# Softmax denominators of an attention stage: adding two steps in float32 before one ones-matmul, with four probability buffers instead of two

## The reference, cut to what matters

```python
def latent_attention(q, k_lat, v_lat, k_ctx, v_ctx):
    scale = 1.0 / math.sqrt(HEAD_DIM)
    k_all = jnp.concatenate([k_ctx, k_lat], axis=1)   # (B, CTX+S, K, d)
    v_all = jnp.concatenate([v_ctx, v_lat], axis=1)
    ...
        s = jnp.einsum('bkgqd,bskd->bkgqs', q_blk, k_all).astype(jnp.float32) * scale
        p = jax.nn.softmax(s, axis=-1).astype(v_all.dtype)
        return jnp.einsum('bkgqs,bskd->bkgqd', p, v_all)
...
        attn = jax.nn.silu(ga) * latent_attention(q, k, v, kc, vc)   # (B, S, ATTN_WIDTH)
        conv = conv_branch(b, cg, hh, gc, conv_w[layer])              # (B, S, CONV_WIDTH)
        y = jnp.concatenate([attn, conv], axis=-1) @ w_out[layer]
        x = x + gate[:, None, :] * y
    return rms_norm(x, final_norm_g)
```

## Time and profile before

| | us |
|---|---|
| runs shown, median | 1207.76 (1199.58 to 1208.54) |
| fastest run shown | 1199.58 |
| span of the profiled execution (slowest core, 7) | 1199.1 |
| spans of its eight cores | 1184.6 to 1199.1 |
| attention stage on core 7, first to last exponential | 722 to 1062 |
| busy in the span: PE, DVE, ACT, POOL | 959.8, 429.3, 505.6, 173.2 |

### The profile page before, as it was taken

The page is one execution under the profiler, slowest core; times in us unless marked ns, Lnnn a source line. Parts: engine busy times, 40 slices in busy tenths (PEclk is TensorE's granted clock), DMA queues, the critical chain, the costliest instruction groups (busy, mean ns, idle before and its releaser), DMA issues.

```text
span 1199.1 us, 16921 instructions; the slowest of 8 cores (1184.6 to 1199.1 us)
## 1 busy us (share of the span) xinstructions
PE 959.8 (80%) x5604; PEld 456.6 (38%) x5604; DVE 429.3 (36%) x782; ACT 505.6 (42%) x902; POOL 173.2 (14%) x180
## 2 busy tenths in 40 slices
PE   0011249796898999999999998798989989889995
PEld 0011125443454444444444443343434334334442
DVE  0000134734756840222222223344444444424554
ACT  0000156435545421000000009699999899942111
POOL 1011002343325520011111110100000000000000
PEclk9999969898899999999999999899999999999998
DMA  9999995595549528888888408810000000021442
GB/s 155 158 157 158 151 165 126 84 226 89 88 72 131 81 36 106 105 106 106 106 106 106 71 1 133 130 20 1 1 1 1 1 1 1 1 106 71 156 174 93
DMA packets 101029, 107.30 MB, mean 89 GB/s; under 512 B 4176, under 2 KB 94672, under 8 KB 98768
## 3 DMA queue, kind: packets, MB, share of 16 engines
q0 software_dynamic: 80640, 73.44, 45.0%
q1 hardware_dynamic: 20304, 32.78, 8.8%
HBM read 171.26 MB, written 8.39 MB: 150 GB/s over the span
## 4 chain that ended last, share of the span: by engine, by line
PE 61%; DMA 25%; DVE 5%; ACT 4%; issue 3%; POOL 1%; DVEq 0%; POOLq 0%; ACTq 0%; SPq 0%
PE PS L818 14%; PE PS L976 9%; DMA R<-w_mod 9%; PE PS L937 8%; PE PS L891 8%; DMA big<-xT 6%; PE PS L915 5%; PE PS L789 5%; DMA wg<-w_mod 4%; DMA R<-w_out 4%; PE PS L707 3%; PE PS L473 3%; DMA R<-w_in 2%; PE PS L465 2%; PE PS L602 1%
## 5 line engine op out<-in xcount | busy, mean ns | idle before, releaser
L927 ACT ACTIVATE work<-PS,smx 128x1024 bf16<-128x1024 f32 x272 | 291.2, 1113 | 21.7 <-DVE work L942 11.7
L818 PE MATMUL PS<-R 128*128 128x512 bf16 x1024 | 228.6, 378 | 0.0
L942 DVE TENSOR_TENSOR work<-work 128x512 bf16<-128x512 bf16 x272 | 127.9, 472 | 170.2 <-ACT work L927 109.3
L937 PE MATMUL PS<-work,V 128*128 128x512 bf16 x544 | 164.3, 384 | 8.8 <-DVE work L902 4.4
L891 PE MATMUL PS<-big,KT 128*128 128x512 bf16 x544 | 163.9, 383 | 0.2 <-ACT work L838 0.2
L818 PEld LDWEIGHTS PS<-R 128*128 128x128 bf16 x1024 | 97.9, 97 | 117.8
L915 PE MATMUL PS<-work,ones_bf 128*128 128x512 bf16 x272 | 104.2, 383 | 30.2 <-DVE work L942 30.1
L976 PE MATMUL PS<-R,big 128*128 128x512 bf16 x512 | 112.5, 383 | 3.9 <-POOL big L907 3.9
L351 PE MATMUL PS<-s_bf,R 128*128 128x2 bf16 x512 | 14.8, 165 | 112.5 <-DMA R<-w_mod 112.5
L473 PE MATMUL PS<-R,big 128*128 128x512 bf16 x384 | 90.6, 391 | 0.0
L833 DVE TENSOR_TENSOR work<-PS,work 128x512 f32<-128x512 f32 x16 | 11.1, 692 | 202.9 <-PE PS L818 177.8
(11 more groups left out here) (118 smaller groups left out, 987.0 us busy)
## 6 DMA issues: line engine op xcount, KB each, us to landing
R<-w_mod POOLq DMA_DIRECT2D x8, 2048.0 KB, 24.1
R<-w_conv POOLq DMA_DIRECT2D x8, 2048.0 KB, 23.2
big<-xT POOLq DMA_DIRECT2D x6, 2048.0 KB, 24.1
big<-xT SPq DMA_DIRECT2D x2, 4096.0 KB, 24.8
wg<-w_mod POOLq DMA_DIRECT2D x8, 1024.0 KB, 25.0
R<-w_out POOLq DMA_DIRECT2D x4, 2048.0 KB, 15.3
big<-xown SPq DMA_DIRECT2D x8, 1024.0 KB, 4.9
out<-big SPq DMA_DIRECT2D x8, 1024.0 KB, 4.2
```

Of the source, the lines that this page charges most:

```text
L818: P.op("tensor", lambda e, wb4=wb4, kc=kc, g=g, tt=tt, b=b: e.matmul(bank(b), wb4[:, kc, g, :], hT_own[:, kc, tt * 512:(tt + 1) * 512], st ...
L927: P.op("scalar", lambda e, sp=sp, pp=pp: e.activation(out=PT[pp], in_=PS[sp][:], func=AF.Exp, scale=sm_scale, bias=smx[:, 2:3]), reads=[ps ...
L937: P.op("tensor", lambda e, ob=ob, chunk=chunk, g=g, pp=pp, cl=cl: e.matmul(bank(ob), V[:, chunk, g * 128:(g + 1) * 128], PT[pp][:, cl * 51 ...
L942: P.op("vector", lambda e, pp=pp, tq=tq: e.tensor_tensor(out=tmpb[tq], in0=PT[pp][:, 0:512], in1=PT[pp][:, 512:1024], op=ALU.add), reads=[ ...
```

## The change

Nothing changes in the score matmuls, the exponentials or the V matmuls, except that the probabilities now go round four buffers. The ones-matmul takes two steps at once:

- In every second step (p odd) DVE adds the two `PT` buffers of the pair, 1024 columns, into one float32 buffer `tsum` (line 925), and then the two halves of `tsum` into `tmpb` (line 930). The 17th step has no partner: there the two halves of `PT` are added directly into `tmpb`, as before.
- The ones-matmul (line 940) follows two steps after, so it exists for 9 steps of a pass.
- The norm is split. `emit_norm_a`, the copy of the V result (line 898), stays in the first step of the next pass. `emit_norm_b`, with the logarithm (904), the exponential (905), the multiplication (907) and POOL's gate product (909), moves with the last ones-matmul to the second step. The multiplication is now written in place into the memory of `o_sb` under the name `o_sb`.

The buffers in `work` are laid out anew, and `W_E` names them.

```diff
-        PT = [work[:, i * 512:(i + 1) * 512].bitcast(BF16) for i in range(2)]
-        tmpb = [work[:, 1024 + i * 256:1024 + (i + 1) * 256].bitcast(BF16) for i in range(2)]
-        accs = [work[:, 1536 + i * 512:1536 + (i + 1) * 512] for i in range(4)]
-        lns_sb = work[:, 1536:2048]
-        o_sb = work[:, 2048:2560]
-        rs_sb = work[:, 3584:4096]
+        PT = [work[:, i * 512:(i + 1) * 512].bitcast(BF16) for i in range(4)]
+        tsum = work[:, 2048:3072]
+        tmpb = [work[:, 3072 + i * 256:3072 + (i + 1) * 256].bitcast(BF16) for i in range(2)]
+        lns_sb = work[:, 3584:4096]
+        o_sb = work[:, 4096:4608]
+        rs_sb = work[:, 4608:5120]
         ot_sb = work[:, 4096:4608]
...
-        W_E = [("PT", 0), ("PT", 1), ("tmpb", 0), ("tmpb", 1), "rs", "ot", "lns", "o_sb"]
+        W_E = [("PT", 0), ("PT", 1), ("PT", 2), ("PT", 3), "tsum", ("tmpb", 0), ("tmpb", 1), "rs", "lns", "o_sb"]
...
-        def emit_norm(it):
+        def emit_norm_a(it):
+            ob = 6
+            P.op("vector", lambda e: e.tensor_copy(out=o_sb, in_=bank(ob)), reads=[psr(ob)], writes=["o_sb"])
+
+        def emit_norm_b(it):
             g, tt, hq = iters[it]
             head = g * 4 + hq
-            ob = 6
             sb_ = 7
             P.op("scalar", lambda e: e.activation(out=lns_sb, in_=bank(sb_), func=AF.Ln), reads=[psr(sb_)], writes=["lns"])
-            P.op("vector", lambda e: e.tensor_copy(out=o_sb, in_=bank(ob)), reads=[psr(ob)], writes=["o_sb"])
             P.op("scalar", lambda e: e.activation(out=rs_sb, in_=lns_sb, func=AF.Exp, scale=-1.0),
                  reads=["lns"], writes=["rs"])
             P.op("vector", lambda e: e.tensor_tensor(out=ot_sb, in0=o_sb, in1=rs_sb, op=ALU.mult),
-                 reads=["o_sb", "rs"], writes=["ot"])
+                 reads=["o_sb", "rs"], writes=["o_sb"])
...
+        nsum = [0]
+        sums = {}
+
+        def emit_tree(idx):
+            it, p = items[idx]
+            if p % 2 == 0 and p != NP - 1:
+                return
+            tq = nsum[0] % 2
+            nsum[0] += 1
+            sums[idx] = tq
+            if p % 2 == 1:
+                pa, pb = (idx - 1) % 4, idx % 4
+                P.op("vector", lambda e: e.tensor_tensor(out=tsum, in0=PT[pa], in1=PT[pb], op=ALU.add),
+                     reads=[("PT", pa), ("PT", pb)], writes=["tsum"])
+                src, sres = tsum, "tsum"
+            else:
+                src, sres = PT[idx % 4], ("PT", idx % 4)
+            P.op("vector", lambda e: e.tensor_tensor(
+                out=tmpb[tq], in0=src[:, 0:512], in1=src[:, 512:1024], op=ALU.add),
+                reads=[sres], writes=[("tmpb", tq)])
 
         def emit_summm(idx):
             it, p = items[idx]
-            tq = idx % 2
+            if idx not in sums:
+                return
+            tq = sums[idx]
             sb_ = 7
-            P.op("tensor", lambda e: e.matmul(bank(sb_), ones_bf[:], tmpb[tq], start=(p == 0), stop=(p == NP - 1)),
+            P.op("tensor", lambda e: e.matmul(bank(sb_), ones_bf[:], tmpb[tq], start=(p == 1), stop=(p == NP - 1)),
                  reads=[("tmpb", tq), "ones_bf"], writes=[psr(sb_)])
...
-            pp = idx % 2
+            pp = idx % 4
...
-            if idx > 0:
-                emit_summm(idx - 1)
-                if items[idx - 1][1] == NP - 1:
-                    emit_norm(items[idx - 1][0])
+            if idx > 1:
+                emit_summm(idx - 2)
+                if items[idx - 2][1] == NP - 1:
+                    emit_norm_b(items[idx - 2][0])
+            if idx > 0 and items[idx - 1][1] == NP - 1:
+                emit_norm_a(items[idx - 1][0])
...
-            tq = idx % 2
-            P.op("vector", lambda e, pp=pp, tq=tq: e.tensor_tensor(
-                out=tmpb[tq], in0=PT[pp][:, 0:512], in1=PT[pp][:, 512:1024], op=ALU.add),
-                reads=[("PT", pp)], writes=[("tmpb", tq)])
+            emit_tree(idx)
+        emit_norm_a(len(iters) - 1)
         emit_summm(len(items) - 1)
-        emit_norm(len(iters) - 1)
+        emit_norm_b(len(iters) - 1)
```

More of the change, by code:

```diff
@@ L905, in emit_norm @@
             P.op("vector", lambda e: e.tensor_tensor(out=ot_sb, in0=o_sb, in1=rs_sb, op=ALU.mult),
-                 reads=["o_sb", "rs"], writes=["ot"])
+                 reads=["o_sb", "rs"], writes=["o_sb"])
             P.op("gpsimd", lambda e: e.tensor_tensor(
                 out=mixT[:, head, tt * 512:(tt + 1) * 512], in0=ot_sb, in1=sga[:, head, tt * 512:(tt + 1) * 512],
-                op=ALU.mult), reads=["ot", "sga"], writes=["mixT"])
+                op=ALU.mult), reads=["o_sb", "sga"], writes=["mixT"])
+        nsum = [0]
[17 more added lines that the diff above has]
+                reads=[sres], writes=[("tmpb", tq)])
         def emit_summm(idx):
             it, p = items[idx]
-            tq = idx % 2
+            if idx not in sums:
+                return
+            tq = sums[idx]
             sb_ = 7
-            P.op("tensor", lambda e: e.matmul(bank(sb_), ones_bf[:], tmpb[tq], start=(p == 0), stop=(p == NP - 1)),
+            P.op("tensor", lambda e: e.matmul(bank(sb_), ones_bf[:], tmpb[tq], start=(p == 1), stop=(p == NP - 1)),
                  reads=[("tmpb", tq), "ones_bf"], writes=[psr(sb_)])
```

## The result

The changed kernel takes 1239.36 us (median of 4 runs, 1234.89 to 1243.17), against 1207.76 for the kernel before (median of 3 runs, 1199.58 to 1208.54). A fourth run of the kernel before (1254.52 us), and every later run in which the cores of one die show a lower granted clock and take some per cent longer whatever the kernel, is left out of the medians and ratios. The ratio on record is 1.0307, 95% interval 1.0251 to 1.0363: 37 us slower, between 30 and 44. The quotient of the two medians, 1.0262 or 32 us, lies inside that interval.

What follows compares the result with a forecast made beforehand. It took PE to bound the pass before and DVE after the change: 23.22 us a pass gave +29.8 us, the start +5.1 and the clock +10, so 1207.76 + 45, stated as 1252 us, range 1226 to 1272.

Steps and rivals of the forecast that it cites:

- The bound: Inside a pass: PE bounds now by 0.07 us a step; with the change DVE does, 2.25 us a pair against ACT's 2.03.
- its sign: Inside the pass: the prediction is wrong if DVE is found waiting for ACT there.
- The pair, 2.25 us: DVE's two dependent additions inside a pass: 1.22 + 0.17 + 0.69 + 0.17 us, the 0.17 being waits on itself.
- The rule of the Trainium skill that a semaphore between DVE operations costs nothing: Rival for DVE's pair: no waits on itself, pairs at ACT's 2.03 us, 1223 to 1233 us in all; chance 0.10.
- The border: Between passes, on late DVE's path: 1.50 us from copy to logarithm, 1.49 to the multiplication, 0.61 to the next addition.
- POOL's collision: At the border: POOL's gate product falls into the short addition and adds 0.83 us a pass, bounds 0 and 1.2.
- The pass: One attention pass, DVE's pairs plus border and POOL: 23.22 us against 20.65 before.
- the forecast of +45: Whole kernel: +34.9 us from passes and start, with +10 us for the clock.
- The start: Start of the attention stage: the second pass's copy waits for POOL's first gate product, third logarithm +5.1 us later.
- The clock: PE idle at the border lowers the granted clock in most passes: +10 us, bounds 0 and 27; full-price rival 1269, chance 0.15.
- The base: Whole kernel: the median before the change, 1207.76 us, to which +45 us was added.
- The faster rivals: Long addition at bfloat16 pace, 0.7 us: 1204 to 1214 us, chance 0.05; also border chain hidden, ACT bound: 1181, chance 0.04.

Runs made afterwards that it cites:

- e1: The changed kernel with the pair sum written in bfloat16 instead of float32, nothing else: 1202.85 us, ratio 0.9996 to the kernel before.
- e5: The changed kernel with two float32 pair buffers, each short addition written behind the next pair's long one: 1211.55 us, ratio 1.0055 to the kernel before.
- e4: The changed kernel with a pass's last ones-matmul and norm put back into the next pass's first step, ahead of the waiting V matmul: 1219.88 us.
- e6: The changed kernel with the gate product written on DVE instead of POOL: 1233.90 us, ratio 1.0245 to the kernel before.
- e7: The changed kernel with score matmuls repeated in early steps of a pass, where PE idles: 1230.78 us, ratio 1.0218 to the kernel before.

## Why the prediction was right, point by point

**The bound.** It said that PE bounds inside a pass by 0.07 us a step, and that DVE takes its place with a dependent pair longer than ACT's. Shown: in the passes with an undisturbed clock, the rows of the change have DVE idle inside the pass only on itself; e1 and e5, which shorten the pair in two different ways, both bring ACT back as the bound. The forecast called itself wrong if DVE were found waiting for ACT inside the pass. That is found, in the nine passes with a fall of the clock: 12 waits, 9.6 us of 300.7. There PE at its lower clock is the bound for a while; the forecast priced that time under the clock, but its sign did not leave room for it.

**The pair, 2.25 us.** Measured 2.19. The two durations were right (1.22 and 0.69), and the wait behind the long addition too (0.17). The wait behind the short one is 0.11. In the order of the program its own semaphore stands last of its two waits, and first in the other case; that the second wait costs the 0.06 is argued from this, not shown.

**The rule of the Trainium skill that a semaphore between DVE operations costs nothing** ("VectorE: DVE Perf Modes", "The DRAIN you can't avoid"). It was kept as a rival against one row. The measured pair and e5 speak against it for operations that depend on each other: 0.17 us after the end instead of 0.09 before it. Whether the semaphore or the dependence costs the time is open, since here the two always come together.

**The border.** From copy to logarithm 1.50 us were expected and 1.48 measured, from logarithm to multiplication 1.49 and 1.42. e4 shows what moving the last ones-matmul and the norm costs: 0.85 us a pass (with a collision that is 0.2 us worse in e4), and the falls of the clock.

**POOL's collision.** 0.83 us were expected and 0.70 measured: the short addition ended 1.56 us after the long one (876.64 to 878.20) instead of 0.86.

**The pass.** 23.22 us expected, 22.58 measured: seven pairs at 0.06 less make 0.4, the collision 0.13, the chain from copy to multiplication 0.09. Over 13 passes this mis-sized term is 8 us of the sum. With 1.6 us of the clock and 0.6 of the start it is why the forecast of +45 was above the +34.6 of the profile.

**The start.** +5.1 us expected, +4.5 measured. The row of the held copy shows the cause (7.63 us idle on POOL), and e6, without the product on POOL, confirms it.

**The clock.** +10 us expected, from half the price of one fall in 11 of 14 passes. It fell 9 times in 13 passes on the slowest core, and e7 prices it at 8.4 us, 0.93 a fall: half of 1.9, as taken. The idle times of PE were 0.56, 1.70 and 1.46 where 0.7, 1.9 and 1.8 were expected. That PE's idleness brings the falls about was argued from one fall; e7 shows that filling it takes them away. But the forecast added the idle times up, and e5 shows that their sum alone decides nothing: 3.4 us without a fall, where e1 falls with 2.7. That the forecast came near the right number of falls is in part luck, and what decides between the two kernels stays open.

**The base.** 1252 was 1207.76 + 45. The median is 1239.36, inside the range of 1226 to 1272. The faster rivals needed a packed rate for the float32 output; it ran at 1.224 us.

## What to carry to other kernels

Before moving work from the bound engine to an idle one, price the dependent chain on the idle engine, with its waits on itself and its loss of packed rate, not its busy share: DVE was at 46% and became the bound with a chain of 2.19 us where ACT needs 2.01. Then ask what the moved step stands behind in each queue at the border of a loop; a late engine turns a hidden chain into a visible one. Where the reduction allows it, keep the intermediate in 16 bits: here the same change with one type exchanged, and two other places mended (the order at the border and the engine of the gate product), is the fastest kernel of all.

## What the runs showed of the hardware that was not expected

- A kernel can gain by giving PE more to do: 14 repeated matmuls a pass kept the granted clock at 1.00 in all 13 passes, on every core, where it fell 7 to 9 times without them, and saved 8.6 us in all (e7).
- The idle time of TensorE at a border does not by its sum tell whether the clock falls: 1.16, 1.70, 0.16 and 0.41 us without a fall on eight cores (e5), and 0.30, 1.70 and 0.67 us with 5 or 6 falls a core (e1).
- Which engine starts first makes a difference where DVE and POOL meet: POOL's product lengthened a short addition by 0.70 us when DVE's long addition had started first, a long one by 0.90 us when POOL had started first (e4); in the first case POOL's own product took 1.94 instead of 1.16 us.
